# Hybrid gMLP, S5 and MoE block on eight cores: input tiles read once and cast on chip, evictions placed by the scheduler, constants reordered, bf16 copies of 16 experts in DRAM

## The reference

```python
proj = rmsnorm(h, norm1) @ w_in            # u, v (512 each), s (512)
o_a = gelu(u) * (w_spatial_masked @ rmsnorm(gelu(v)) + b)     # in chunks of 128 tokens, 8 heads
# o_b: complex diagonal scan over the sequence, 32 groups x 64 states, then gelu and a gated linear
a_bar = exp(lam * dt);  states = scan(a_bar, ((a_bar - 1) / lam) * b_mat @ s)
o_b = glu(gelu(real(c_mat @ states) + d_skip * s))
h = h + concat(rmsnorm(o_a), rmsnorm(o_b)) @ w_out
h = h + moe(rmsnorm(h, norm2))             # 32 experts of 1024 x 256 x 1024, 2 for each token
h = h + sigmoid(rmsnorm(h, norm3) @ w_ple_gate) * (p @ w_ple_proj)
out = rmsnorm(h, final_norm)
```

## Time and profile before

| | us |
|---|---|
| Median of 3 runs | 1279.25 (1276.35 to 1282.11) |
| The profiled execution | 1273.09 |
| Its span on its slowest core | 1271.2 |
| Spans of the eight cores | 1242.5 to 1271.2 |
| PE, DVE, ACT, POOL busy | 830.8, 638.9, 522.6, 469.8 |

### The profile page before, as it was taken

One profiled execution on the slowest core, in us unless ns is written; L12 is line 12 of the kernel. 1 busy time (PEld: TensorE's weight loads), 2 busy tenths in 40 slices (PEclk: granted clock), 3 DMA queues, 4 the chain that ended last, 5 costly groups with the idle time before them and its releaser, 6 DMA issues.

```text
span 1271.2 us, 19834 instructions; the slowest of 8 cores (1242.5 to 1271.2 us)
## 1 busy us (share of the span) xinstructions
PE 830.8 (65%) x5475; PEld 522.7 (41%) x5475; DVE 638.9 (50%) x1065; ACT 522.6 (41%) x816; POOL 469.8 (37%) x555
## 2 busy tenths in 40 slices
PE   2576959778759986894356656666557628057773
PEld 1245727444324334564345444444435416023331
DVE  5975291478881331445614443433334424249992
ACT  2574223667634742232005443432435424136552
POOL 1777462145420220110154332423324312127874
PEclk9785579999986997997668887877778869578886
DMA  8996122975246669756127885954866981588832
GB/s 181 220 236 175 42 33 37 236 162 126 67 77 128 169 127 225 244 191 133 36 90 251 272 283 186 314 195 144 298 243 224 271 225 39 141 279 263 271 138 84
DMA packets 72390, 224.33 MB, mean 176 GB/s; under 512 B 17563, under 2 KB 21659, under 8 KB 63780
## 3 DMA queue, kind: packets, MB, share of 16 engines
q1 hardware_dynamic: 43348, 165.27, 40.2%
q0 software_dynamic: 28880, 57.20, 22.1%
HBM read 227.11 MB, written 58.72 MB: 225 GB/s over the span
## 4 chain that ended last, share of the span: by engine, by line
PE 42%; DMA 23%; DVE 13%; issue 13%; ACT 4%; POOL 3%; SPq 1%; DVEq 1%; POOLq 1%; ACTq 0%
PE p L527 35%; DMA yd<-t,t 8%; PE p L531 7%; DVE t L491 6%; DMA t<-xnd,t 4%; DVE t L501 3%; DVE t L521 3%; DMA t<-xprev 2%; DMA hd<-t 2%; ACT t L515 2%; DMA t<-w_pg 2%; POOL t L491 1%; ACT t L519 1%; DMA t<-gvec 1%; DMA t<-x 1%
## 5 line engine op out<-in xcount | busy, mean ns | idle before, releaser
L527 PE MATMUL p<-t,t 128*128 128x512 bf16 (+9 forms) x3843 | 701.0, 341 | 125.0 <-DVE t L491 53.9
L527 PEld LDWEIGHTS p<-t,t 128*128 128x128 bf16 (+5 forms) x3843 | 394.1, 128 | 387.2 <-issue 240.6
L531 PE MATMUL p<-t,t 128*128 128x128 bf16 (+1 forms) x1632 | 161.7, 255 | 294.5 <-DVEq L436 111.6
L531 PEld LDWEIGHTS p<-t,t 128*128 128x128 bf16 (+1 forms) x1632 | 132.4, 117 | 339.9 <-issue 322.0
L491 POOL TENSOR_TENSOR t<-t,t 128x1 f32<-128x1 f32 (+2 forms) x195 | 217.1, 1119 | 90.6 <-DVE t L491 25.6
L521 DVE COPY t<-p 128x1024 bf16<-128x1024 bf16 (+2 forms) x196 | 127.9, 666 | 206.6 <-PE p L531 104.1
L519 ACT COPY t<-p 128x512 f32<-128x512 f32 (+2 forms) x180 | 124.5, 706 | 187.0 <-DMA yd<-t,t 72.9
L515 ACT ACTIVATE t<-t 128x1024 bf16<-128x1024 f32 (+2 forms) x147 | 132.4, 901 | 144.6 <-DVE t L491 78.1
L501 DVE SCALAR_TENSOR_TENSOR t<-t,t,t 128x1024 f32<-128x1024 f32 (+3 forms) x97 | 136.0, 1428 | 86.2 <-POOL t L491 54.6
L491 DVE TENSOR_TENSOR t<-t,p 128x512 f32<-128x512 f32 (+2 forms) x116 | 85.7, 757 | 156.9 <-PE p L527 90.8
L491 DVE TENSOR_TENSOR t<-t,t 128x512 f32<-128x512 f32 (+10 forms) x238 | 144.2, 632 | 18.8 <-PE p L527 4.2
(11 more groups left out here) (32 smaller groups left out, 200.2 us busy)
## 6 DMA issues: line engine op xcount, KB each, us to landing
t<-wall SPq DMA_DIRECT2D x66, 1024.0 KB
t<-x SPq DMA_DIRECT2D x48, 512.0 KB, 5.3
t<-yd SPq DMA_DIRECT2D x32, 512.0 KB, 5.7
t<-wall POOLq DMA_DIRECT2D x10, 1536.0 KB, 19.4
t<-xprev SPq DMA_DIRECT2D x16, 512.0 KB, 7.8
t<-x POOLq DMA_DIRECT2D x32, 256.0 KB, 4.6
hd<-t SPq DMA_DIRECT2D x16, 512.0 KB, 5.0
t<-hd SPq DMA_DIRECT2D x16, 512.0 KB, 8.7
```

The source lines that it names most:

```text
L527: self.add("pe", lambda e: e.matmul(out.ap, lhsT=lhsT.ap, rhs=rhs.ap, start=start, stop=stop), reads=list(lhsT.keys) + list(rhs.keys), pwr ...
L531: self.add("pe", lambda e: e.transpose(out=out.ap, in_=a.ap, identity=ident.ap), reads=list(a.keys) + list(ident.keys), pwrites=list(out.k ...
```

## The change

1. `front_parts` loads a tile once, in float32; DVE or ACT casts it to bf16. 48 casting DMAs go, 48 casts of 128x1024 come.
2. A new method `either` gives an operation two forms, for DVE and for ACT, and `arrange` takes the engine that is free first in its count. It is used for these casts and for most evictions of segment 0.
3. S5 constants: PN is kept for both halves (QM shares PX), all P come first, then the chain R, then both halves of Q. The 64-row matmuls of MT and of `yunit` alternate between the upper and the lower 64 rows, with one PSUM bank each, and form one group.
4. `conv` copies the weights of expert k, k = 0 to 15, from `wall` to a bf16 tensor `wbd` in DRAM, in one casting DMA of POOL (3.1 MB read, 1.6 MB written). Copy k is tied to the row mean of tile q = 16 + 2k. The keys are `("wb", e)`.
5. `W0` to `W9` are loaded from `wbd`, still by POOL; experts 10 to 15 are loaded from `wbd` by SP in the steps 0 to 5 of the expert loop. Float32 pieces remain for experts 16 to 31, 48 in place of 66, the first cast point at step 6.
6. The routing's buffers lie elsewhere.

```diff
+        def offer(i):
+            for e in (ulist[i][0].alt or (eng[i],)):
+                avail.setdefault(e, []).append(i)
...
+            if ulist[pick][0].alt:
...
+                eng[pick] = op.eng = e
+                op.fn, cost[pick] = op.alt[e]
...
+    def either(self, out, a, scale=None, pw=False):
...
+        alt = {"dve": (dve, self._c("dve", n, 0.63 if scale is None else 0.85)), "act": (act, self._c("act", n, 1))}
...
+    def wbf(e_):
+        return V(wbd[e_].rearrange("(p n) -> p n", p=128), ("wb", e_))
+
+    def conv(e_, mark):
+        P.dma(wbf(e_), I["wall"][e_ * WSZ:(e_ + 1) * WSZ].rearrange("(p n) -> p n", p=128), q="pool", cls="w0", after=(mark,), max_dma_last_dim=8192)
...
-    PN = [P.tile(list(S4), F32, es=sa_) for _ in range(2)]
+    PNs = [[P.tile(list(S4), F32, es=sa_) for _ in range(2)] for _ in range(2)]
...
-    QM = [P.tile(list(S4), F32, es=sa_) for _ in range(2)]
+    QM = PX
...
+    CONV = {16 + 2 * k_: k_ for k_ in range(NCV)}
+
     def front_parts(src_of, q):
         xs_ = next_xf()
         P.dma(xs_, src_of)
-        P.dma(hx[q % 3], src_of, q="pool")
-        mean_sq(xs_, 1024, col(ssA, q), col(rsA, q))
+        P.either(hx[q % 3], xs_)
+        m_ = mean_sq(xs_, 1024, col(ssA, q), col(rsA, q))
+        k_ = CONV.get(q)
+        if k_ is not None:
+            conv(k_, m_)
...
+    for e_ in (4, 5, 6, 7, 0, 1, 2, 3, 8, 9):
         P.claim(("W", e_), HEND + e_ * 12288, HEND + (e_ + 1) * 12288)
...
+        P.dma(wring[:, e_ * 6144:(e_ + 1) * 6144].rk(("W", e_)), wbf(e_), q="pool", cls="w0")
...
-    pieces = [(e_, j) for e_ in range(NB, NE) for j in range(3)]
+    pieces = [(e_, j) for e_ in range(NCV, NE) for j in range(3)]
...
+        if NB + e_ < NCV:
+            P.dma(ring[:, e_ * 6144:(e_ + 1) * 6144].rk(("W", e_)), wbf(NB + e_), cls="out")
```

More of the change, by code:

```diff
@@ L523, in mm @@
     def mm(self, out, lhsT, rhs, start, stop):
-        if start:
+        if start and not self.hold:
             self.grp += 1
@@ L547, in dma @@
         which = dict(pwrites=wk) if (pw or not isinstance(out, V)) else dict(writes=wk)
-        size = 4
+        size = 2 if oap.dtype == BF16 and iap.dtype == BF16 else 4
         for d in oap.shape:
             size *= d
-        self.add(q, lambda e: e.dma_start(out=oap, in_=iap, **kw), reads=rd, is_dma=True, cls=cls, size=size, cost=(1000 if q == "pool" else 400), **which)
+        self.add(q, lambda e: e.dma_start(out=oap, in_=iap, **kw), reads=rd, is_dma=True, cls=cls, size=size, extra_deps=after, cost=(1000 if q == "pool" else 400), **which)
     def gather(self, out, table, idx, most, cls="gat"):
@@ L850, in build_program @@
                 gp0 = part * 8 + q2 * 2
[L851 to L854, removed]
-                sh = (128, 8, n) if n == 64 else (128, 16, n)
-                for hs in ((slice(0, 8), slice(8, 16)) if n == 64 else (slice(0, 16),)):
-                    cmul(Rr[:, hs, n:2 * n], Ri[:, hs, n:2 * n], Rr[:, hs, 0:n], Ri[:, hs, 0:n],
-                         Rr[:, hs, n - 1:n].bc(sh), Ri[:, hs, n - 1:n].bc(sh), sh, split=n >= 32)
-                n *= 2
+                P.either(PT[:, gp0:gp0 + 2, i1], pt_.re("p (a b) c -> p a b c", a=2), pw=True)
+    n = 1
+    while n < 128:
+        sh = (128, 8, n) if n == 64 else (128, 16, n)
+        for hs in ((slice(0, 8), slice(8, 16)) if n == 64 else (slice(0, 16),)):
+            cmul(Rr[:, hs, n:2 * n], Ri[:, hs, n:2 * n], Rr[:, hs, 0:n], Ri[:, hs, 0:n],
+                 Rr[:, hs, n - 1:n].bc(sh), Ri[:, hs, n - 1:n].bc(sh), sh, split=n >= 32)
+        n *= 2
+    for part in range(2):
+        gs = par(part)
+        PN = PNs[part]
         cmul(QN[0], QN[1], pwr[:, gs].us(3).bc(S4), pwi[:, gs].us(3).bc(S4), cre[:, gs].us(2).bc(S4), cim[:, gs].us(2).bc(S4), S4, neg=True)
@@ L883, in build_program @@
+                    P.hold = False
+                for h in range(2):
+                    dst = MT.re("p (q h) a c -> p h q a c", h=2)[:, h, p0:p0 + 4, off, :]
+                    if off:
+                        P.either(dst, pms[h], pw=True)
+                    else:
+                        P.tt(dst, pms[h], maskM.us(1).bc((128, 4, 128)), ALU.mult, pw=True)
         QX = PX
@@ L1247, in build_program @@
     lo_ = rt([128, 32]); P.stt(lo_, hi_, -128.0, slot.re("p k t -> p (k t)"), ALU.mult, ALU.add)
-    OHlo = [rt([128, 8, 128]) for _ in range(4)]
+    es_r2 = Mem(*A_QT)
+    OHlo = [P.tile([128, 8, 128], F32, None, es=es_r2) for _ in range(4)]
     RH = [rt([128, 8, NCOL]) for _ in range(4)]
```

121 lines of the change are left out of this document (70 added, 51 removed).

## The result

The changed kernel takes 1301.1 us (median of 4 runs, 1295.5 to 1308.9) against 1279.7: 1.018 times as long, 95% interval 1.013 to 1.023. The forecast was 1225, faster. The profiled execution has a span of 1307.4 us on its slowest core, here core 3.

What follows compares the result with a forecast made beforehand. Bounds by stretch: DVE and PE alternating in the constants, DVE in gMLP, PE busiest in 373 to 587 us. Terms -28 + 8 - 5 - 10 - 20 = -55 from 1279.25 gave 1224, stated as 1225; range 1185 to 1285.

Steps and rivals of the forecast that it cites:

- the copies: gMLP stage: the serial chain of weight copies takes 119 us against 111, +8 us (0 to +50).
- The distance c: Time from one chained copy to the next on POOL, taken as 16 us, near the lower end of 14.6.
- the last of the things that would make the prediction wrong: Copies delaying the S5 tiles between 90 and 234 us, left at nothing beyond the quarter given back.
- R3: Rival, slower: the copy chain holds POOL; loses if the gMLP stage ends after 408 us; 1341 at c = 24; chance 0.14.
- 110 + 15c: Time in us when the chain of copies ends the gMLP stage, if later than 353; c is the copy-to-copy time.
- R1: Rival: a copy is limited by its bytes on both sides, 18.2 us from copy to copy; 1255 us; chance 0.22.
- The constants and MT: Front of the kernel: parallel 64-row pairs and a shorter DVE gap give -38, a quarter given back, -28 us (0 to -50).
- R2: Rival: the 64-row pairs of MT and the S5 output do not run side by side; 1245 us; chance 0.10.
- The casts at nothing: gMLP stage: on-chip casts of tiles taken as no cost, up to 11 us if the scheduler's guess is wrong.
- S5 output, -5: Stage after the gMLP tiles: weight loads leave and products alternate, PE at clock 0.58 stays; -5 us (0 to -10).
- Output projection, -10: Weight loads spread over the stage in place of a burst of four; -10 us of 21 (0 to -20).
- Experts, -20: First six expert steps take 8.5 us each in place of 11.8, later steps gain nothing; -20 us (0 to -35).

Runs made afterwards that it cites:

- e2: The changed kernel without copies: experts 0 to 9 by casting loads from float32 weights, 10 to 31 as float32 pieces; 1226.6 us, ratio 0.961.
- e1: The changed kernel with a key of its own for each copy, so no copy waits for the one before it; 1266.6 us, ratio 0.989.
- f3: The kernel before with only the 64-row products of MT and the S5 output alternating between upper and lower rows; 1237.5 us, ratio 0.968.
- e5: The changed kernel without copies, with 64-row products of MT and `yunit` one half of the rows after the other; 1279.9 us, ratio 1.003.
- e6: The changed kernel without copies, with bf16 tiles loaded by POOL's casting DMAs as before, not cast on chip; 1222.9 us, ratio 0.959.
- f4: The changed kernel without copies, with the old product order in `yunit`, so pairs in MT alone; 1235.1 us, ratio 0.969.

## Why the prediction was wrong

**The term that failed is the copies:** the sum gave them +8 us. Against e2, which has none, the changed kernel is 78 us late at the gated linear and 72 at the end, though the end holds what they give in the expert loop. Three errors are in the term.

- *The price of a copy.* I took 9.4 us of all DMA engines, the casting load's, as "the nearest row", and 14.6 as the other end. It is 12.1 to 12.9 (the changed kernel, e1), in the middle of these ends. The distance c was taken as 16; 18.4 in the gMLP tiles and 20.7 over all were measured. (The end of the range "+50 (c = 20)" fits neither rule of the prediction: 7 x 20 + 7 is 36 over 111, and 110 + 300 is 57 past the forecast 353.)
- *The place.* The sum charged the copies only in the gMLP stage. Eight of them were issued before it, and the stretch from the end of MT to the first gMLP product went from 46 to 99 us (e2: 54). This was named as the last of the things that would make the prediction wrong, and it should have been in the sum: 16 x 12 = 194 us of all DMA engines had to fit between 105 and 415 us.
- *The volume apart from the wait.* The rivals priced the chain of waits only. e1, where no copy waits for another, is still 36 to 40 us behind e2; its DMA share is 0.93 to 0.99 and a tile takes 12.3 us to land, not 4.0.

**The formula of R3 was right, its chance too small.** 110 + 15c with c = 20.7 gives 421 for the end of the gMLP tiles; it was 429 (and 436 on the slowest core, where this c was measured and the first copy went at 105 us, not at about 90). The break-even of 408 was passed by 21, and the result is 21 us slower; that the two agree to the microsecond is luck, since behind the tiles the S5 output gave 26 us and the projection none, where 5 and 10 were forecast. R3, the serial chain, had 0.14, and I had weighed the 19.4 us landing of the casting loads down because those "ran together or beside tile loads". The copies landed in 19.0 us: they run beside tile loads too, and the one that ran nearly alone still took 15.1.

**R1** gave 18.2 us for the copies in the gMLP tiles, and 18.4 were measured, but the engines' time in a copy is 12.1 us and not 14.6. With 12.1 its own sum gives 15.7, so the agreement is luck. Its support was misread too: the earlier trace rows show 212 GB/s at most, not 222, and the page of before has slices of up to 314. No run here told whether it is the bytes on both sides that set a copy's time.

**The constants and MT:** -28 net by 262 us was forecast, and without the copies it came: the first spatial product stands 27 us earlier in e2, 28 in f3. For the end of MT the sum had +5 for the later start, -15 and -8 for the two blocks and -20 for the gap between them, -38 in all; e2 has +10.5, -18.5, -8.7 and -18.6, -35 in all.

Two things in it are right by luck. The first block was to gain by the pairs alone, and of the 26 us that PE was busy less with it (40.6 to about 15), about 17 are the clock, by an estimate: at 1.00 the like block without pairs takes 24 us (the second half, before), so the pairs gave 9 in each block, and the rest went because the block no longer ran at 0.50. And the gap, which the order of the constants was to shorten, shrank by 19 us in e2 and by 7 in f3, yet f3 reaches the gMLP tiles at the same time as e2: what the order gives at MT's end is gone by then. The order was never run alone, so its worth is not shown; e5 has it without the pairs and gains nothing.

What the prediction left out is that the clock changes with the pairing. In before it was 0.50 throughout the first block, 40 us of PE busy, on every core; in e5 it fell to 0.50 within 6 us of the block's start and stayed there to its end; in the changed kernel it was at 1.00, or rose to it within 11 us. It is not the unpaired products alone that hold it down: the second block of before had them too and ran at 1.00. And in the paired kernels bf16 products stand among MT's, which may have helped.

**R2,** pairs that don't run side by side, is excluded: 23 instructions against 11 in one microsecond at the same clock.

**The casts at nothing** stands: e6, without them, is 4 us faster, which the spread of the runs does not tell from no change. In the first 113 us the DMA share fell from 0.88 to 0.49 and the stage, bound by DVE, had no use for it.

**S5 output, -5:** the stretch behind the gMLP tiles fell from 42 to 15 us in the changed kernel and 16 in e2; this term was 20 us too small, which is what e2 gained beyond its expectation. The prediction had left it at PE's clock of 0.58. The pairs in it give 3.5 us at the clock 1.00 (f4 against e2). In f3 all its products stand behind the tiles, as before, and it takes 24.5 us at a clock of about 0.82, so 17 us go without any shift of work. In e2 18 of its 64 products of 64 rows stand among the last gMLP tiles, in the changed kernel 48. How the rest divides between clock and shift stays open; it wasn't tried.

**Output projection, -10:** about 0. The first three steps became even, as said, and the later ones long: the weight loads, released one by one by the stores of `hd`, only moved there. In e2, with casting loads, the stage takes 134 us, so bf16 sources gain 3 us at most.

**Experts, -20:** -16 by the cores' medians, of which e2 has 2 without any copies; e1, with the same loads, has 7. A step took 9.1 to 10.7 us and not 8.5; the sum by DMA time (7.3 us) was not the bound.

## What to carry to other kernels

A transfer moved off a stage's path isn't free where it lands: add up the DMA engines' time over the whole stretch from its first issue to its last use, and compare it with the idle share there, before looking at who waits. Here each copied expert moved 12 us of DMA time into the front to save about 1 us in the loop. When a change bundles parts, one part may carry all of the gain: the order of two loops over 64-row products is worth 41 us by itself, and the copies around it turned that into a loss. And count single instructions before a stage is said to begin: a merged row had put the start of the gMLP tiles 7 to 15 us late.

## What the runs showed of the hardware

- A casting copy from DRAM to DRAM ran at 122 to 130 GB/s of bf16 written (1.573 MB in 12.1 to 12.9 us of all 16 engines), a casting load into SBUF at 166 to 167.
- Beside such copies the hardware queue moved 251 GB/s of its own busy time (e1), beside casting loads only 307 (e2), and a tile load landed in 12.3 us against 4.0.
- 64-row float32 instructions of one half of the rows start 112 ns apart at the clock 1.00. When they alternate between the two halves, in two PSUM banks, those of the other half run in the same time: 23 against 11 in one microsecond. A row of 32 takes 2.24 us against 3.50. Where full-row and 64-row products follow each other, the next start comes after 0.20 us.
- The first block of unpaired products ran at the granted clock 0.50 (1.2 GHz) on every core of before, with PE busy throughout for 40.6 us, and in e5 from its first 6 us on; the second block of before ran at 0.99 to 1.00 with PE as busy. In the changed kernel, with pairs, the first block was at 1.00 from its start on five cores and within 11 us on the others. What sets this stays open.
